# First two layers of a four-layer block stack: the gate is projected last, convolution steps stand among the rotary steps, the time-step columns ride with keys and values, and the turns of keys and queries stand inside the last projection

## The reference, cut to what matters

```
h = rms_norm(x, norm_mix_w[i])
proj = jnp.einsum("bld,de->ble", h, w_in[i])
q, k, v, z, xbc_raw, dt_raw = jnp.split(proj, split_at, axis=-1)   # 512,128,128,512,1024,16
q = rms_norm(q.reshape(b, l, N_Q_HEADS, HEAD_DIM), q_norm_w[i])    # k likewise, 2 heads
q = axial_rope(q, cos_r, sin_r, cos_c, sin_c)                      # k likewise
attn_out = blocked_gqa(q, k, v)                                    # full attention, 8 heads
xbc = jax.nn.silu(depthwise_conv_centred(xbc_raw, conv_w, conv_b)) # 5 taps
dt = jax.nn.softplus(dt_raw + dt_bias)
# state-space scan over x, B, C with dt, then y * silu(z), group norm
x = x + jnp.einsum("ble,ed->bld", jnp.concatenate([attn_out, ssd_out], -1), w_out[i])
```

## Time and profile before

| what | value |
|---|---|
| median of three runs | 2561.71 us |
| the profiled execution | 2568.79 us |
| its span, first to last instruction | 2566.9 us |
| granted PE clock over the span | 0.979 |
| PE busy | 2460.0 us, 96% |
| DVE busy | 1488.2 us, 58% |
| ACT busy | 932.3 us, 36% |

### The profile page before, as it was taken

The page is one execution under the profiler, slowest core; times in us unless marked ns, Lnnn a source line. Parts: engine busy times, 40 slices in busy tenths (PEclk is TensorE's granted clock), DMA queues, the critical chain, the costliest instruction groups (busy, mean ns, idle before and its releaser), DMA issues.

```text
span 2566.9 us, 30991 instructions
## 1 busy us (share of the span) xinstructions
PE 2460.0 (96%) x12524; PEld 2008.3 (78%) x12524; DVE 1488.2 (58%) x2116; ACT 932.3 (36%) x1424; POOL 210.7 (8%) x141
## 2 busy tenths in 40 slices
PE   7989999999998999999998889999999888999999
PEld 6767888888876788888886668888888666888887
DVE  5867543435586754343558676646465876655544
ACT  4464422223336432222343543222234364322222
POOL 2001200000200120000132002000012201100000
PEclk9989999999998999999999899999999999999999
DMA  4100222222220022222322002222232200322222
GB/s 177 67 34 1 83 99 99 99 99 99 99 83 18 1 84 97 99 99 99 107 90 99 2 1 94 90 96 98 99 115 99 82 2 3 109 98 89 98 98 99
DMA packets 30238, 205.32 MB, mean 80 GB/s; under 512 B 3344, under 2 KB 3728, under 8 KB 6032
## 3 DMA queue, kind: packets, MB, share of 16 engines
q1 hardware_dynamic: 30096, 203.35, 22.5%
HBM read 201.24 MB, written 2.10 MB: 79 GB/s over the span
## 4 chain that ended last, share of the span: by engine, by line
PE 88%; DVE 7%; DVEq 2%; ACT 2%; issue 1%; DMA 0%; POOL 0%; ACTq 0%; SPq 0%
PE bank L1449 25%; PE bank L1451 25%; PE bank L1450 25%; PE bank L1599 2%; PE bank L1575 2%; PE bank L1556 2%; PE bank L1531 1%; DVE a_conv L969 1%; PE bank L1794 1%; PE bank L1742 1%; DVE w_lo L713 1%; DVE b_p L1324 1%; PE bank L1586 1%; PE bank L1909 1%; DVE neg_max L1312 1%
## 5 line engine op out<-in xcount | busy, mean ns | idle before, releaser
L713 DVE TENSOR_TENSOR w_lo<-w_raw,w_hi 128x2048 fp32r<-128x2048 f32 (+1 forms) x190 | 433.9, 2284 | 415.5 <-ACT w_hi L318 415.4
L1449 PE MATMUL bank<-h_ffn_hi,w_hi 128*128 128x512 f32 x1408 | 548.6, 390 | 0.0
L1451 PE MATMUL bank<-h_ffn_hi,w_lo 128*128 128x512 f32 x1408 | 547.8, 389 | 0.0
L1450 PE MATMUL bank<-h_ffn_lo,w_hi 128*128 128x512 f32 x1408 | 547.7, 389 | 0.0
L318 ACT ACTIVATE w_hi<-w_raw 128x2048 fp32r<-128x2048 f32 (+1 forms) x190 | 360.0, 1895 | 506.2 <-PE bank L1451 457.4
L1451 PEld LDWEIGHTS bank<-h_ffn_hi,w_lo 128*128 128x128 f32 x1408 | 264.3, 188 | 54.9
L1450 PEld LDWEIGHTS bank<-h_ffn_lo,w_hi 128*128 128x128 f32 x1408 | 264.3, 188 | 54.7
L1449 PEld LDWEIGHTS bank<-h_ffn_hi,w_hi 128*128 128x128 f32 x1408 | 264.3, 188 | 54.6
L1449 PE MATMUL bank<-act_hi,w_hi 128*128 128x512 f32 x704 | 273.9, 389 | 0.0
L1450 PE MATMUL bank<-act_lo,w_hi 128*128 128x512 f32 x704 | 273.9, 389 | 0.0
L1451 PE MATMUL bank<-act_hi,w_lo 128*128 128x512 f32 x704 | 273.9, 389 | 0.0
(11 more groups left out here) (296 smaller groups left out, 3448.8 us busy)
## 6 DMA issues: line engine op xcount, KB each, us to landing
w_raw<-weights SPq DMA_DIRECT2D x188, 1024.0 KB, 4.7
residual<-x_in SPq DMA_DIRECT2D x8, 256.0 KB, 6.1
x_out<-residual SPq DMA_DIRECT2D x8, 256.0 KB, 2.0
cst<-consts SPq DMA_DIRECT2D x1, 960.0 KB, 10.5
par_b<-params_b SPq DMA_DIRECT2D x1, 627.0 KB, 11.5
par_a<-params_a SPq DMA_DIRECT2D x1, 244.0 KB, 2.7
w_raw<-weights SPq DMA_DIRECT2D x2, 64.0 KB, 1.9
```

What stands on the lines that cost most here:

```text
L713: nc.vector.tensor_tensor(w_lo[s][:, cols], w_raw[s][:, cols], w_hi[s][:, cols].bitcast(F32), ALU.subtract).then_inc(w_ready, 1)
L1449: mm(out, ahi, bhi, start=start, stop=False)
L1450: mm(out, ahi, blo, start=False, stop=False)
L1451: return mm(out, alo, bhi, start=False, stop=stop)
```

## The change

Six edits, all in the input part of the two layers and the head of their attention:

1. The groups come in another order: queries (g0, g0+1), keys with values and the 16 time-step columns, 272 wide, in two groups of four k-tiles (g0+2, g0+3), convolution channels (g0+4 to g0+7), gate z last (g0+8, g0+9). The number of groups stays ten.
2. ACT evicts keys, values and time steps together (`evict_kv`); the group of the time steps with its copy and small turns is gone.
3. On DVE `conv_start` 0 and 1 stand among the rotary steps, and the last rotary step stands after `conv_start(7)`.
4. On PE the turns of the convolution channels stand later (0 and 1 together in the middle of g0+6, 2 and 3 in g0+7, 4 and 5 in g0+8); two key turns and two query turns stand in the middle of the last projection group, in four different banks; two query turns stand after it.
5. The attention waits for its queries step by step instead of for all at its head, and the query tiles are 2 to 5 of `h_mix` instead of 4 to 7; some scratch tiles change place for that.
6. Group g0+10 is split at step 6 of the attention, and g0+11 at step 8.

```diff
@@ scalar engine, per layer
+                def evict_kv(half):
+                    g = g0 + 2
+                    act.wait_ge(bank_done, done_with(g + 1, half))
+                    for t in (2 * half, 2 * half + 1):
+                        j = pair_bank(g, t)
+                        for dst, at, n in ((A["a_k"][:, t, :], 0, P), (A["a_v"][:, t, :], P, P), (A["a_dt"][:, 0, 16 * t:16 * t + 16], 2 * P, 16)):
+                            nc.scalar.activation(dst, bank[j][:, at:at + n], ACT.Copy, scale=rstd[:, t:t + 1])
+                        nc.scalar.activation(A["a_squares"][:, t, 512:640], bank[j][:, 0:P], ACT.Square,
+                                             scale=rstd[:, t:t + 1]).then_inc(bank_free[j], 1)
+                        act.drain().then_inc(hsq_done, 1)
+                    act.drain().then_inc(qk_raw, 1)
...
-                act.wait_ge(bank_done, done_with(g0 + 9, 0))
-                nc.scalar.activation(sq[0][0:16, :], bank[2][0:16, :], ACT.Copy).then_inc(bank_free[2], 1)
...
+                conv_middle(0)
+                split_hi(g0 + 6)
+                conv_middle(1)
+                conv_act(0)
+                split_hi(g0 + 7)
+                conv_act(1)
+                conv_middle(2)
...
+                conv_act(6)
+                for m in range(4):
+                    turned_hi(m)
+                evict_z(0)
+                conv_act(7)
+                evict_z(1)
+                for m in (4, 5):
+                    turned_hi(m)
...
-                    if i == 6:
-                        split_hi(g0 + 11)
+                    if i in (6, 8):
+                        split_hi(g0 + 7 + i // 2)
@@ vector engine, per layer
+                rope_a(0)
+                dve.wait_ge(hsq_done, 8 * lay + 8)
...
+                split_lo(g0 + 5)
+                rope_a(1)
+                dve.wait_ge(dt_s, 2 * lay + 1)
+                nc.vector.tensor_scalar(dt[2], dt[1], 1.0, None, ALU.add).then_inc(dt_v, 1)
+                conv_start(0)
+                rope_a(2)
+                conv_start(1)
...
@@ matrix engine, per layer
+                for second in range(2):
+                    enter(g0 + 2 + second)
+                    for half in range(2):
+                        pair_half(g0 + 2, second, half, width=KVD)
+                        if second == 0 and half == 0:
+                            broadcast(2 * lay)
...
+                        feature_half(g0 + 4 + g, half, h_mix_hi, h_mix_lo, KT)
+                        if g == 2 and half == 0:
+                            turn_channels(0)
+                            turn_channels(1)
+                        if g == 3:
+                            turn_channels(2 + half)
+                for second in range(2):
+                    enter(g0 + 8 + second)
+                    for half in range(2):
+                        pair_half(g0 + 8, second, half)
+                        if second == 0:
+                            turn_channels(4 + half)
+                        elif half == 0:
+                            pe.wait_ge(rope_ready, 4 * lay + 4)
+                            pe.wait_ge(xt_free, 6 * lay + 6)
+                            for m in range(2):
+                                turn_key(m)
+                            for m in range(2):
+                                turn_query(m)
+                turn_query(2)
+                turn_query(3)
...
-                for j in range(4):
-                    open_bank(j, g0 + 10)
-                pe.wait_ge(t_free, base + 6)
...
+TURN_A = (5, 6, 7, 4, 7, 4, 5, 6, 5, 6)
```

More of the change, by code:

```diff
@@ L827, in tile_lo @@
                 dve.wait_ge(t_hi_done, base + count + 1)
-                src = bank[5 + count % 2][:, :]
+                src = bank[turn_bank(base, count)][:, :]
                 if scale is None:
@@ L974, in conv_taps @@
                     last.then_inc(conv_out, 1)
[L976 to L983, removed]
-                conv_taps(7)
-                for m in range(2):
-                    tile_lo(m, 10 * lay, h_mix_hi[:, m, :], h_mix_lo[:, m, :])
@@ L990, in _ @@
[L990 to L995 removed]
+                dt = [A["a_dt"][:, j, :] for j in range(7)]
@@ L998, in _ @@
+                conv_taps(3)
+                split_lo(g0 + 8)
+                conv_start(5)
+                conv_taps(4)
+                conv_start(6)
+                conv_taps(5)
+                conv_start(7)
+                split_lo(g0 + 9)
+                rope_a(3)
+                conv_taps(6)
                 for m in range(4):
-                    tile_lo(2 + m, 10 * lay, h_mix_hi[:, 4 + m, :], h_mix_lo[:, 4 + m, :])
-                    if m == 1:
-                        dve.wait_ge(dt_s, 2 * lay + 1)
-                        nc.vector.tensor_scalar(dt[2], dt[1], 1.0, None, ALU.add).then_inc(dt_v, 1)
+                    turned_lo(m)
@@ L1004, in finish_dt @@
+                conv_taps(7)
+                for m in (4, 5):
+                    turned_lo(m)
                 def finish_dt():
@@ L1470, in token_half, with pair_half @@
                 last.then_inc(bank_done, 1)
-            def pair_half(g, second, half, n=None):
+            def pair_half(g, second, half, n=None, width=2 * COLS):
                 s = (g + second) % 2
@@ L1526, in turn @@
             def turn(count, base, src):
-                if count >= 2:
-                    pe.wait_ge(t_free, base + count - 1)
+                j = turn_bank(base, count)
+                earlier = [n for n in range(count) if turn_bank(base, n) == j]
+                if earlier:
+                    pe.wait_ge(t_free, base + earlier[-1] + 1)
                 for t in range(TB):
-                    last = nc.tensor.transpose(bank[5 + count % 2][:, t * P:(t + 1) * P], src(t), ident)
+                    last = nc.tensor.transpose(bank[j][:, t * P:(t + 1) * P], src(t), ident)
                 last.then_inc(t_done, 1)
@@ L1707, in _ @@
-                enter(g0 + 9)
-                open_bank(2, g0 + 9)
-                for k in range(KT):
-                    ws = slice(k * 16, (k + 1) * 16)
-                    last = three(bank[2][0:16, :], w_hi[1][:, ws], w_lo[1][:, ws], h_mix_hi[:, k, :], h_mix_lo[:, k, :],
-                                 k == 0, k == KT - 1)
-                last.then_inc(bank_done, 1)
-                base = 10 * lay
-                pe.wait_ge(rope_ready, 4 * lay + 4)
-                pe.wait_ge(xt_free, 6 * lay + 6)
@@ L1916, in width_of, with turn_bank @@
 def width_of(g):
-    return KT * 16 if g in (FIRST[0] + IN_A - 1, FIRST[1] + IN_A - 1) else GW
+    return 4 * KVD if g in [FIRST[lay] + n for lay in range(LAYERS) for n in (2, 3)] else GW
+def turn_bank(base, count):
+    return TURN_A[count] if base < 20 else (5, 6)[count % 2]
 def tiny_wide(B):
@@ L1985, in _layer @@
     every = slice(None)
-    parts, at = [], 0
-    for width in plan:
-        cs = slice(at, at + width)
-        if width == 2 * COLS:
+    parts = []
+    for cs in plan:
+        if len(cs) > COLS:
             parts += [("in", w_in, cs, slice(n * D_MODEL // 2, (n + 1) * D_MODEL // 2)) for n in range(2)]
```

139 lines of the change are left out of this document (73 added, 66 removed).

## The result

The changed kernel takes 2545.8 us (median of 4 runs, 2544.8 to 2547.0) against 2565.0 (4 runs, 2561.4 to 2570.7) for the kernel before, run beside it: ratio 0.9923, interval 0.9909 to 0.9938. The forecast was 2538 with a range of 2526 to 2553, and 2533 to 2545 for its likeliest case: the result lies in the range, and 0.8 us above that case. The profiled execution took 2545.49 us with a span of 2543.7, that of before 2568.79 with 2566.9: 23.2 us less in the span, which is the forecast sum. The medians differ by 19.2 only, since the profiled execution of before lay above its own median.

What follows compares the result with a forecast made beforehand. PE, busy for 96% of the span, was taken to bound the kernel. Two layers of −12.3 us at the landmark and +0.7 behind it gave −23.2 us, from 2561.7 to 2538.5 us; range 2526 to 2553.

Steps and rivals of the forecast that it cites:

- forecast sum: Whole kernel: two layers of −12.3 + 0.7 = −11.6 us, together −23.2 us.
- likeliest case: Whole kernel: the forecast case by itself, 2533 to 2545 us, chance 0.58.
- PE without waits: Input part: time-step group's 5.64 us go, wider operands +0.6, four turns +1.9; last projection half ends at 123.7 us.
- New waits: PE in the convolution groups: 0.3 us at the split of g0+6, 2.0 at the second convolution turn; net 2.1.
- The fourth rival (the ring): Convolution turns one place late: PE waits some 4 us at turns 1, 2, 3, clock falls; 2588 us, chance 0.05.
- The landmark: First maximum of layer one's attention: 129.1 instead of 141.43 us, gain 12.3 us; the same taken for layer two.
- The third rival: Head of attention: wait not removed, landmark at 134 to 136 us, 6 us gained a layer; 2550 us, chance 0.09.
- The second split, +0.7 us a layer: In the attention: one PE wait of 0.73 us for the copy behind it, +0.7 us a layer.
- upper end of 2.4: In the attention: upper bound for the second split's cost, its full length of 2.4 us.
- Clock, nothing gained: Behind the landmark: the second slow stretch falls again, no gain counted; upper bound of what may return 8.5 us.
- forecast 2.1 us wait before the second turn: Head of attention: PE's wait for the copy of the first turned probabilities stays, 2.1 us.
- first rival: Attention: clock stays up or returns sooner, up to 8.5 us more, 2530; half likelier, 2534 us; chance 0.15.

Runs made afterwards that it cites:

- e4: Changed kernel with all four rotary steps on DVE before the first `conv_start`, all else kept; 2557.34 us, ratio 0.9974 to the kernel before.
- e3: Changed kernel with the two key turns and two query turns back behind the last projection group; 2556.57 us, ratio 0.9963 to the kernel before.
- e12: Changed kernel with its turns behind the last projection and all rotary steps before the first `conv_start`; 2566.84 us, ratio 1.0002 to the kernel before.
- e1: Changed kernel with g0+10 split before the attention, in DVE's gap before the key turns, and only g0+11 in the attention; 2537.92 us.
- e2: Changed kernel with the second convolution turn moved from the middle to the end of group g0+6 on PE; 2540.42 us.
- e5: Changed kernel with the edits of e1 and e2 together; 2534.20 us, ratio 0.988 to the kernel before.
- e7: Changed kernel with its second split at step 10 of the attention instead of step 8; 2541.33 us.
- e10: Kernel before with one unused 128x512 matmul in the input part of layer one; 2564.47 us, ratio 0.9994.
- e9: Kernel before with two unused 128x512 matmuls in the input part of layer one; 2566.63 us, ratio 1.0002.
- e8: Kernel before with the time-step copy and two high key parts ahead of `conv_act(7)` on ACT; 2558.28 us, ratio 0.9973.

## Why the prediction was right, and where two of its terms were wrong

1. **PE without waits.** 24 matmuls of 272 columns take 42.59 − 39.57 = 3.02 us, 126 ns each against 122: +0.4 us for 96, forecast 0.6. Those two starts:

```profile
39.57 0.28 PE L1488 MATMUL bank<-w_hi,h_mix_hi 128*128 128x272 f32 x1
...
42.59 1.05 PE L1562 MATMUL bank<-cst,rstd 128*128 128x128 f32 x8
```

The Trainium skill, "TensorE: Matmul & The Clock Gate", section "Wait — 56ns, not 53.3ns?", gives columns by 2.4 GHz plus 2.5 ns from start to start, 116 ns as an estimate. The trace does not agree (126), and it decides.

2. **New waits.** 0.3 us at g0+6 (0.28) and 2.0 at the second turn (1.79), none at turns 2 to 5 or at later splits: as forecast. e4 shows how tight the first is. The fourth rival (the ring) did not come: from 82.74 us on nothing waits.

3. **The landmark.** The last half ends at 125.09 (125.8), and 3.44 us later (3.3) stands the first maximum: 128.53 against 129.1. This execution was 0.47 us ahead before any changed instruction, since the clock rose earlier in its first projection, so the gain is 12.4 us; forecast 12.3. In layer two it is 25.58 − 12.74 = 12.8 (12.74 us are gained when layer two begins). e3, e4 and e12 show of what it is made: the turns 5.6, the rotary order 6.4 (with the fall of the clock that its wait brings), and neither hides the other's wait. The third rival is out: no taps stand between the gate's half and the last low parts.

4. **The second split, +0.7 us a layer: wrong.** It costs 4.36 and 3.48 us (e1). The term took the wait that the split of step 6 leaves for one at step 8. There the split stands behind another operation on ACT, so that two waits come. Where the clock stays up behind them they cost 2.1 us (layer one, e12 against e1: 63.94 and 61.86) to 2.5 (layer two, e2 against e5: 63.89 and 61.35), about the upper end of 2.4. The rest in layer one is the fall of the clock behind them, which the term did not have. In layer two the clock does not fall at step 8: of the 3.48 us 2.6 lie there, and 0.9 at the slow stretch from 761.2 us. At step 10 (e7, layer one) the split leaves one wait of 0.74 us, as the term had it.

5. **Clock, nothing gained: wrong, the other way.** The second slow stretch of the kernel before is gone in both layers. With the split out of the way (e1) the stretch is 4.19 and 2.56 us shorter than before, though the wait before the third scores grew to 3.12 us as forecast (2.7). The clock did fall again, but while PE waits or the maxima and exponentials set the pace. The forecast 2.1 us wait before the second turn is not there: PE reaches it late, DVE waiting 0.6 us for its scores. The first rival named the mechanism with its bound of 8.5 us; 6.8 came. But e10 and e9 show the old order without that slow stretch too, 4.6 and 3.1 us shorter, so its loss is not owed to the new order alone. Why the clock falls a second time in one execution and not in another stays open.

6. **The sum was right by cancellation.** Terms 4 and 5 together are +0.17 and +0.92 us, forecast 0.7 each. At layer two's first scan product 24.66 us are gained, and 23.2 at the end. The difference is lost at one place of the unchanged code, in the input part of layer three: behind the same wait the clock stayed up in the kernel before and fell in the changed one. PE's row behind the wait and its clock there, before:

```profile
1331.98 0.50 PE L1449 MATMUL bank<-w_hi,h_mix_hi 128*128 128x512 f32 x1 [2.71 <-DVE w_lo L713]
1333.00:1340.00 7.00, 7.00 (x32) 1.00 0.76 295
```

and after:

```profile
1307.31 0.67 PE L1488 MATMUL bank<-w_hi,h_mix_hi 128*128 128x512 f32 x1 [2.71 <-DVE w_lo L744]
1307.20:1310.60 3.40, 3.29 (x8) 0.54 0.66 212
```

Behind it the gain is 23.1 us. So it is luck that the spans differ by exactly the forecast 23.2.

7. **From the sum to the median: 7.3 us off.** The forecast put the median as far below the profiled execution as it lay before, by 7.1 us. The changed kernel's profiled execution (2545.49) lies at its median (2545.8). For the kernel before 3 runs gave 2561.7, and 17 to 25 runs 2564 to 2567. Forecast from the profiled execution alone, the time would have been 2545.6.

## What to carry to other kernels

A split or copy that moves into a busy loop is priced by what stands ahead of and behind it in that step's queue, not by the wait that its twin leaves in another step. Before a wait is removed, look at the engine that would be late next, since the named releaser may hide it: dropping the group, with the old orders on DVE and PE, gained nothing that could be measured. Where a difference of up to 5 us lies in code that was not touched, compare the granted clock there first; several executions of one kernel, and kernels shifted by one matmul, tell whether an order deserves the credit.

## What was not expected of the hardware

The same instructions behind the same waits took 66.05 or 61.43 us, with or without a second slow stretch of the clock, and behind the same wait of 2.71 us in layer three the clock fell in one execution and not in the other. One exchange of two steps on ACT (e8) took 7.1 us off the median of ten runs, of which some 2 us a layer are explained by its own waits; the rest is open. And a weight split of 1.91 us on ACT and 2.29 on DVE, both under 60% busy, cost PE up to 4.4 us, of which 2.1 to 2.5 are its waits.
